# DeltaNet phase: products kept for the other direction, decays and triangles of two steps made in the tail of the step before

## The reference

```
S_t = exp(g_t)(I - beta_t k_t k_t^T) S_{t-1} + beta_t k_t v_t^T ;  o_t = S_t^T q_t
o_f, s_f = gated_delta_scan(dq, dk, dv, beta[:, :, 0], g[:, :, 0], dn_s0[:, 0])
o_b, s_b = gated_delta_scan(flip(dq), flip(dk), flip(dv), flip(beta[:, :, 1]), flip(g[:, :, 1]), dn_s0[:, 1])
o_dn = o_f + flip(o_b)
```

## Time and profile before

| | |
|---|---|
| median of 3 runs | 3465.98 us (3464.9 to 3468.81) |
| the profiled execution | 3469.74 us |
| its span in the trace | 3468.0 us |
| TensorE, VectorE, ScalarE, GpSimd busy | 3281.3, 2291.9, 1768.7, 298.5 us |
| step 1 of the DeltaNet phase, first turn to first turn | 1447.26 to 1511.61 |
| first turn of step 0; the next phase's start | 1388.43; 1699.95 |

### The profile page before, as it was taken

The page is one execution under the profiler, slowest core; times in us unless marked ns, Lnnn a source line. Parts: engine busy times, 40 slices in busy tenths (PEclk is TensorE's granted clock), DMA queues, the critical chain, the costliest instruction groups (busy, mean ns, idle before and its releaser), DMA issues. The chain is left out here.

```text
span 3468.0 us, 48349 instructions
## 1 busy us (share of the span) xinstructions
PE 3281.3 (95%) x19680; PEld 2709.8 (78%) x19680; DVE 2291.9 (66%) x2436; ACT 1768.7 (51%) x2260; POOL 298.5 (9%) x302
## 2 busy tenths in 40 slices
PE   5899998999999999999979999959999999999995
PEld 0799998989999998999869998846666666666663
DVE  1587547656665666445574352678888888888886
ACT  2455323323433233666573233537777777777774
POOL 0000000001100001311212000010000100100000
PEclk8999999999999999999989999979999999999997
DMA  9422323545455553312436333869999999999998
GB/s 414 164 91 84 148 111 123 178 165 187 169 185 185 177 184 107 77 38 74 122 86 211 121 132 134 308 228 349 390 399 396 376 395 398 386 384 395 396 372 324
DMA packets 176358, 794.42 MB, mean 229 GB/s; under 512 B 17460, under 2 KB 70068, under 8 KB 96948
## 3 DMA queue, kind: packets, MB, share of 16 engines
q1 hardware_dynamic: 158180, 699.81, 54.0%
q0 software_dynamic: 17136, 86.91, 7.6%
q10 hardware_dynamic: 864, 5.27, 0.4%
HBM read 729.48 MB, written 62.46 MB: 228 GB/s over the span
## 5 line engine op out<-in xcount | busy, mean ns | idle before, releaser
L2557 DVE TENSOR_TENSOR expert_lo<-expert_ring,first_expert_hi 128x2048 fp32r<-128x2048 f32 x288 | 660.0, 2292 | 111.7 <-ACT first_expert_hi L2494 108.0
L2494 ACT ACTIVATE first_expert_hi<-expert_ring 128x2048 fp32r<-128x2048 f32 x285 | 546.9, 1919 | 175.0 <-PE bank L2441 175.0
L2440 PE MATMUL bank<-expert_lo,xeT_hi 128*80 128x512 f32 x1024 | 402.1, 393 | 0.0
L472 PE MATMUL bank<-h_hi,part_hi 128*128 128x320 f32 x960 | 301.6, 314 | 8.2 <-DVE part_lo_x L860 4.5
L2439 PE MATMUL bank<-first_expert_hi,xeT_hi 128*80 128x512 f32 x768 | 303.2, 395 | 1.2 <-DVE xeT_lo L2562 1.2
L2441 PE MATMUL bank<-first_expert_hi,xeT_lo 128*80 128x512 f32 x768 | 299.2, 390 | 0.0
L472 PE MATMUL bank<-h_lo,part_hi 128*128 128x320 f32 x960 | 298.2, 311 | 0.0
L860 DVE TENSOR_TENSOR part_lo_x<-part_x,part_hi 128x1024 fp32r<-128x1024 f32 x120 | 149.3, 1245 | 152.7 <-ACT part_hi L684 145.5
L2557 DVE TENSOR_TENSOR expert_lo<-expert_ring,expert_hi 128x2048 fp32r<-128x2048 f32 x96 | 219.6, 2287 | 43.5 <-ACT expert_hi L2494 43.5
L684 ACT ACTIVATE part_hi<-part_x 128x1024 fp32r<-128x1024 f32 x120 | 127.3, 1061 | 217.3 <-PE bank L472 197.6
L472 PE MATMUL bank<-s_hi,part_hi 128*128 128x320 f32 x720 | 226.7, 315 | 4.0 <-DVE part_lo_x L860 4.0
(11 more groups left out here) (406 smaller groups left out, 7630.5 us busy)
## 6 DMA issues: line engine op xcount, KB each, us to landing
expert_ring<-d_wgate SPq DMA_DIRECT2D x128, 1024.0 KB, 7.3
expert_ring<-d_wup_e SPq DMA_DIRECT2D x128, 1024.0 KB, 7.8
expert_ring<-d_wdown SPq DMA_DIRECT2D x128, 1024.0 KB, 10.3
mod_slot<-d_wmod SPq DMA_DIRECT2D x56, 1024.0 KB, 6.7
part_b<-d_win SPq DMA_DIRECT2D x90, 512.0 KB, 3.2
front_ring<-d_wmod SPq DMA_DIRECT2D x40, 1024.0 KB, 8.3
front_ring<-d_win SPq DMA_DIRECT2D x29, 1024.0 KB, 4.8
d_proj<-out_rows POOLq DMA_DIRECT2D x86, 320.0 KB, 2.4
```

The costliest lines, as they stand in the source:

```text
L472: mm = pe.matmul(part_bank[j][:, 0:HALF_T], w, a[:, kk, :], start=(kk == 0 and x == 0), stop=(kk == HALF_K - 1 and x == 2))
L2440: pe.matmul(out[0:CAP, :], a_hi, lo, start=False, stop=False)
L2494: act.activation(w_hi[n % NSPLIT][:], w[:, n % NSLOT].rearrange("p (k n) -> p k n", n=HALF), ACT.Copy).then_inc(s["we_high"], 1)
L2557: dve.tensor_tensor(w_lo[n % NSPLIT][:], w[:, n % NSLOT].rearrange("p (k n) -> p k n", n=HALF), w_hi[n % NSPLIT][:].bitcast(F32), ALU.subt ...
```

## The change

- Step 0 makes kT, vT, KK and QK once for both directions (quads 0 and 2). VectorE does the halves of level 0 of a pair straight behind its triangles.
- Steps 1 and 2 make them for all four quads. ScalarE then copies KK out of PSUM into `keys_keys` (which takes R's place) and QK into `vnew`, eight copies of 128x512. The triangles read `keys_keys`, and scoresT reads `vnew` and is made behind the halves of level n = 2. R is written over `vtok`.
- SP stores V, KK and QK of step 1 and V and QK of step 2 in HBM (`d_keep`, 20 DMAs of 256 KB), and brings them back for the other direction: V and QK of step 2 in step 3, the three of step 1 in step 4 (20 DMAs). KK of step 2 stays in SBUF. Values are fetched no more for steps 3 and 4.
- Steps 3 and 4 leave out kT, vT, KK and QK. Their decay rows, decays, triangles and first strips are made in the tail of the step before (EARLY_HEADS): the decay rows behind XTend on TensorE, the decays behind the XT copies on ScalarE, the triangles between R and the O/S updates on VectorE. QS of quads 1 and 3 is done ahead of the levels.

The diff, cut to its core:

```diff
+def dn_left_out(q):
+
+    return {FIRST_STEP: ("QS", "KS", *(FRESH if q % 2 else ())), 3: FRESH, LAST_STEP: (*FRESH, "S")}
+EARLY_HEADS = (3, 4)
...
+                for q in range(4):
+                    B[q].wait_emptied(sp, 1, "vT")
+                    keep(KEEP_V1, q, vtok)
+                for q in range(4):
+                    A[q].wait_emptied(sp, 1, "KK")
+                    keep(KEEP_KK1, q, KK)
+                for q in range(4):
+                    B[q].wait_emptied(sp, 1, "QK")
+                    keep(KEEP_QK1, q, vn)
+                next_keys(2)
...
+                next_keys(3)
+                sp.wait_ge(spilled, SPILLED[2])
+                for q in range(4):
+                    A[q].wait_filled(sp, 2, "P")
+                    bring(KEEP_V2, q, vtok, v_back)
+                for q in range(4):
+                    A[q].wait_filled(sp, 2, "O")
+                    bring(KEEP_QK2, q, vn, qk_back)
+                for p in range(2):
+                    sp.wait_ge(LT_made[p], 4)
+                for q in range(4):
+                    bring(KEEP_KK1, q, KK, kk_back)
+                next_keys(4)
...
                             if n == 1:
-                                A[2 * p].wait_emptied(pool, step, "KK")
-                                A[2 * p + 1].wait_emptied(pool, step, "KK")
+                                pool.wait_ge(LT_made[p], step + 1)
...
+                    fresh = {0: QUADS[0::2], 1: QUADS, 2: QUADS}.get(step, ())
...
+                    if step not in EARLY_HEADS:
+                        decay_rows(step)
...
+                    if not fresh:
+                        for q, d, h0 in QUADS[1::2]:
+                            wait_rows(step, d, landed)
+                            queries_state(step, q, d, h0, x)
...
                         turn(A[q], step, "XTend", lambda h: (E, O)[d][p][0][:, h, :])
+                    if step + 1 in EARLY_HEADS:
+                        decay_rows(step + 1)
...
+                    for q in range(4 if step in (1, 2) else 0):
+                        A[q].wait_filled(act, step, "KK")
+                        act.activation(KK[q][:], h4(A[q].t[:]), ACT.Copy).then_inc(A[q].emptied, 1)
+                    for q in range(4 if step in (1, 2) else 0):
+                        B[q].wait_filled(act, step, "QK")
+                        act.activation(vn[q][:], h4(B[q].t[:]), ACT.Copy).then_inc(B[q].emptied, 1)
...
+                    if step + 1 in EARLY_HEADS:
+                        decays(step + 1)
+                    if step in SPILLED:
+                        act.wait_ge(spilled, SPILLED[step])
...
+                def triangles(step, p):
+                    for q, d, h0 in QUADS[2 * p:2 * p + 2]:
+                        if step == FIRST_STEP:
+                            A[q - d].wait_filled(dve, step, "KK")
+                            keys = h4(A[q - d].t[:])
+                        else:
+                            if step < 3:
+                                A[q].wait_emptied(dve, step, "KK")
+                            elif step == 4:
+                                dve.wait_ge(kk_back, 64)
+                            keys = KK[keys_of(step, q)][:]
+                        A[q].wait_emptied(dve, step, "G")
+                        for h in range(4):
+                            c = d * 8 + h0 + h
+                            op = dve.scalar_tensor_tensor(
+                                out=NT[p][:, 1 - d, h, :], in0=keys[:, h, :],
+                                scalar=col(k.beta[:], tile_at(step, d), c, c + 1), in1=DT[q][:, h, :],
+                                op0=ALU.mult, op1=ALU.mult)
+                    if step == FIRST_STEP:
+                        op.then_inc(A[2 * p].emptied, 1)
+                    dve.drain().then_inc(LT_made[p], 1)
+                    cut(dve, p, 0).then_inc(first_strip[p], 1)
...
+                        if step > FIRST_STEP and n == 2:
+                            for q, d, h0 in QUADS:
+                                if step < 3:
+                                    B[q].wait_emptied(dve, step, "QK")
+                                else:
+                                    dve.wait_ge(qk_back, 64 * (step - 2))
+                                dve.tensor_tensor(sc[q][:], vn[q][:], DT[q][:], ALU.mult)
...
+                            if step < 3:
+                                dve.wait_ge(spilled, SPILLED[step])
+                            else:
+                                dve.wait_ge(v_back, 64 * (step - 2))
...
                     dve.drain()
+                    if step + 1 in EARLY_HEADS:
+                        for p in range(2):
+                            triangles(step + 1, p)
```

More of the change, by code:

```diff
@@ L85, with __init__ @@
 class Bank:
-    def __init__(self, tensor, filled, emptied, fills, left_out):
+    def __init__(self, tensor, filled, emptied, names):
         self.t, self.filled, self.emptied = tensor, filled, emptied
-        names = [(step, f) for step in range(TT) for f in fills if f not in left_out.get(step, ())]
         self.before = {name: n for n, name in enumerate(names)}
@@ L103, in wait_emptied, with in_steps @@
         wait(eng, self.emptied, self.before[step, fill] + 1)
+def in_steps(fills, left_out):
+    return [(step, f) for step in range(TT) for f in fills if f not in left_out.get(step, ())]
 class Chip:
@@ L985, with a_names @@
 FIRST_STEP, LAST_STEP = 0, TT - 1
[L986 removed]
+FRESH = ("kT", "vT", "KK", "QK")
+KEEP_V1, KEEP_KK1, KEEP_QK1, KEEP_V2, KEEP_QK2 = range(5)
+def dn_left_out(q):
+    return {FIRST_STEP: ("QS", "KS", *(FRESH if q % 2 else ())), 3: FRESH, LAST_STEP: (*FRESH, "S")}
 B_FILLS = [["vT", "QK"] + [f"XY{s}" for s in LEVELS[1:]] + ["QS", "S"], ["vT", "QK", "QS", "S"]]
+EARLY_HEADS = (3, 4)
+def a_names(q):
+    names = in_steps(A_FILLS[q % 2], dn_left_out(q))
+    for step in EARLY_HEADS:
+        names.remove((step, "G"))
+        names.insert(names.index((step - 1, "XTend")) + 1, (step, "G"))
+    return names
 def columns(ap, s, other, heads=P):
@@ L1015, in phase_deltanet @@
         ktok, vtok, DT, sc = (quads(n) for n in ("ktok", "vtok", "decayT", "scoresT"))
-        XT, R, vn, vs = (quads(n) for n in ("XT", "R", "vnew", "vweighted"))
+        XT, KK, vn, vs = (quads(n) for n in ("XT", "keys_keys", "vnew", "vweighted"))
         NT = [sb(f"LT{p}", [P, 2, 4, P]) for p in range(2)]
@@ L1075, in _, with keep @@
                              ).then_inc(k.ml_first_in, 16)
[L1076 to L1083, removed]
+                def keep(slot, q, src):
+                    sp.dma_start(k.d_keep[slot, q], src[q][:].rearrange("p h n -> p (h n)")).then_inc(spilled, 16)
@@ new lines, in bring, with next_keys @@
+                def bring(slot, q, dst, back):
+                    sp.dma_start(dst[q][:].rearrange("p h n -> p (h n)"), k.d_keep[slot, q ^ 1]).then_inc(back, 16)
+                def next_keys(step):
+                    for d in range(2):
+                        sp.wait_ge(used[d], step * 2)
+                        fetch(step, (step, TT - step), d, 0, 16, landed)
+                for d in range(2):
+                    B[2 + d].wait_filled(sp, 1, "vT")
+                    fetch(2, (2, TT - 2), d, 16, 24, v_landed)
@@ L1124, in turn, with wait_rows, queries_state, decay_rows @@
                     mm.then_inc(bank.filled, 1)
[L1126 to L1137, removed]
+                def wait_rows(step, d, arrived):
+                    pe.wait_ge(arrived[0 if step == FIRST_STEP else d], 16 if step == FIRST_STEP else 16 * (step + 1 - d))
+                def queries_state(step, q, d, h0, x):
+                    fill(B[q], step, "QS", lambda h: [(staged[d][:, h0 + h, :], S[x][q][:, h, :])])
+                def decay_rows(step):
                     for q, d, h0 in QUADS:
@@ new lines, in body @@
+                    for p in range(2):
+                        if step not in EARLY_HEADS:
+                            triangles(step, p)
+                        if step == FIRST_STEP:
+                            halves(step, 0, p)
+                    for n in range(len(LEVELS)):
+                        for p in range(2):
+                            if step > FIRST_STEP or n > 0:
+                                halves(step, n, p)
+                        if step == FIRST_STEP and n == 0:
+                            for q, d, h0 in QUADS:
+                                B[q - d].wait_filled(dve, step, "QK")
+                                op = dve.tensor_tensor(sc[q][:], h4(B[q - d].t[:]), DT[q][:], ALU.mult)
+                                if d == 1:
+                                    op.then_inc(B[q - 1].emptied, 1)
+                        if step > FIRST_STEP and n == 2:
[5 more added lines that the diff above has]
+                                dve.tensor_tensor(sc[q][:], vn[q][:], DT[q][:], ALU.mult)
```

137 lines of the change are left out of this document (77 added, 60 removed).

## The result

The changed kernel takes 3483.42 us (median of 5, 3483.01 to 3485.3), the kernel before, beside it, 3466.59: ratio 1.0049, interval 1.0037 to 1.0062. It is slower by 17 us; forecast were 3466.6 and a range up to 3475. The profiled execution has a span of 3481.2, of before 3468.0.

What follows compares the result with a forecast made beforehand. TensorE was taken to set the pace, with VectorE the bound in the changed tails of steps 3 and 4. Gains of 11.0 us less 9.8 for VectorE-GpSimd meetings and 1.8 for clock gave -0.6: median 3466.6, range 3455 to 3475.

Steps and rivals of the forecast that it cites:

- The triangles of the second pair wait for one strip at most: VectorE's second-pair triangles, steps 1 to 4, wait for one GpSimd strip over SBUF: 1.2 us each, 4.8 together.
- The carry copies: Steps 3 and 4: four VectorE copies meet GpSimd's back-to-back strips, two passing per gap: 1.7 us a step, 3.4 together.
- second rival: GpSimd retakes the port after every VectorE instruction; copies and scores wait a strip each: 9.2 us slower, 3475; chance 0.17.
- The clock: TensorE's gaps in the heads of steps 3 and 4 lower its clock: 1.8 us for one head, bounds 0 and 3.6.
- a sign that all of it is wrong: The whole forecast is wrong if the six levels no longer take 30.85 us.
- Step 0: Sixteen turns and 16 products go, ScalarE has four copies fewer: gain 1.5 us, bounds 0 and 2.7.
- the interleaving: Step 0: second pair's triangles stand some 1.4 us behind the first pair's turn and halves; some 1.0 less after the last strip.
- Steps 1 and 2: First level begins later because ScalarE copies KK behind the decays: a loss of 1.1 us each, 2.2 together.
- the 2.0 us of KK behind the decays: Steps 1 and 2: triangles start 2.0 us later, as ScalarE's first KK copy comes after the decays.
- The scores: Steps 1 and 2: free in second-level gaps at 2.48 us; meeting GpSimd's strips costs 0.8 each, 1.6 together, bounds 0 to 2.0 each.
- Steps 3 and 4 without contention: XTend's end to first level takes 26.95 us, from 33.5 into step 3: gains 6.55 and 4.8, together 11.4.
- Transfers: Added 256 KB DMAs and dropped v fetches cost nothing, each issued at least 20 us ahead of use.

Runs made afterwards that it cites:

- second run: Changed kernel with GpSimd's strips started only behind VectorE's first strip of the second pair: 3476.65 us, ratio 1.0030 to the kernel before.
- first experiment: Changed kernel with GpSimd's first strip of a pair waiting for VectorE's strip of that same pair: 3476.34 us, ratio 1.0029 to the kernel before.
- third run: Changed kernel with the four carry copies of steps 3 and 4 moved to the begin of the tail before: 3473.36 us, ratio 1.0022.
- fifth: Changed kernel with GpSimd behind both VectorE strips and the carry copies at the begin of the tail before: 3462.15 us, ratio 0.9989.
- sixth: The fifth run's kernel; in steps 1 and 2 triangles read KK from PSUM and scores come behind level 3: 3453.99 us, ratio 0.9966.
- ninth run: The eighth run's kernel plus two fills of unread products on TensorE between step 0's two XY1 turns: 3448.91 us, ratio 0.9948.
- seventh run: The sixth run's kernel with step 0's halves of level 0 behind both pairs' triangles again: 3454.02 us, ratio 0.9966.
- eighth run: The seventh run's kernel; VectorE adds the state's part of quads 1 and 3 to o_dn during levels 1 and 2, steps 3 and 4: 3450.79 us.
- repetition: The eighth run's kernel measured once more, unchanged: 3450.92 us.

## Why the prediction was wrong

**The step that failed** is "The triangles of the second pair wait for one strip at most ... 1.2 in each of four steps, 4.8". I had the resource right and the meeting wrong. GpSimd is released by the triangles, ahead of VectorE's own strip, and got the port first; so both of VectorE's strips wait, in every step, step 0 too, 1.15 each (to the next start: 1460.45 to 1462.33 is 1.88, 1456.71 to 1457.44 was 0.73): 11.5 us, not 4.8. The triangles waited for nothing (2.17). Without these waits the heads were 9.1 us shorter (second run, the cast left aside). I read in the earlier trace rows that GpSimd's strip waited for VectorE's and did not ask what the 0.05 us that set this order would be after the edit. The first experiment puts the wait where I had forecast it, at about 1.1 in each of four steps. The Trainium skill's rule (SBUF — State Buffer, "Who interferes with whom") has it that whoever issues first keeps the port for a whole instruction; GpSimd's strip of 1.31 and VectorE's of 1.95, with starts 0.01 apart, agree.

**The carry copies** were the right place at half the price: 4.45 us for 0.85, so 3.6 a head, where I took 1.7. Moving them away shortened the two heads by 8.0 us in all, their own time included (third run). GpSimd let one copy by at a time; that was the second rival's mechanism, and its 3.9 was near. Its 3475 still was 8 too low, for want of the strips.

**The clock** was charged once, 1.8 us. The first level became longer in all five steps, together 6.7; the prediction had named levels that are no longer 30.85 as a sign that all of it is wrong. I had looked for gaps in the heads of steps 3 and 4 alone. They came in steps 0 to 2 as well, and the late strips widened them: TensorE waited 4.97, 3.48 and 3.48 us there for the second pair's first strip, and 3.80, 1.41 and 1.41 in the second run. Each gap closed by an edit gave its levels 30.8 again (third, fifth, sixth and ninth run).

**Step 0**: forecast 1.5 faster; the head is 1.7 slower, 1.25 from the first turn on. Two strips wait (2.3), and the interleaving costs 1.5 in the head (seventh run), where I had counted 1.4 less 1.0. Without both, the head is 1.7 faster than before the change (21.86 for 23.58), near the forecast. Behind it come 1.0 more in the levels at the lower clock.

**Steps 1 and 2**: the 2.0 us of KK behind the decays was right (triangles 9.28 behind the first turn, 7.20 before) and came back in the sixth run. The first level, for which I counted 1.1 a step, came 1.9 later in the second run, where TensorE also waited 0.78 for GpSimd's first strip. The scores cost nothing in the change, in step 1 by 0.16 us; where they meet the strips they take 2.75 and 2.43 longer, above the 2.0 of my bound, and TensorE waits 1.50 and 1.18 of it.

**Steps 3 and 4 without contention**: forecast 26.95 for the stretch, 26.1 without the copies' 0.85; 25.86 in the fifth run, where the copies are out of it. The early heads and the missing products are worth what was counted, and the collisions ate it.

**Transfers**: nothing, as forecast. No wait of the phase in the trace ends with one of them, and of the edits that gave the time back none touched them, but for KK's return, which is released one strip later.

## What to carry to other kernels

When a change moves an instruction of VectorE that reads two tiles of SBUF, or a copy, into a stretch in which GpSimd works, price it at a whole GpSimd instruction for each one that is met, and look which of the two is released first, down to hundredths of a microsecond. A release that stands one instruction too early can cost about what the change saves: here 9 us in the heads, where the early heads, freed of the meetings, are worth 10. Releasing GpSimd only when VectorE's last such instruction is done cost 0.9 us in step 0, and in the last versions nothing in the others; look what else it then meets, as the scores did in the second run. Then look for the gaps that such waits open on TensorE, in every step, since what follows can be paid at a lower clock.

## What was not expected of the hardware

- The start of VectorE's and GpSimd's strips lay 0.05 us apart before and 0.01 the other way after, and the later one paid: 0.6 us (GpSimd) or 1.1 (VectorE).
- Behind a train of strips VectorE's copies of 0.3 us advance by one per strip, 1.27 apart, while VectorE's O/S updates in the same train, with one input in PSUM, keep their 0.67 and 1.11 us.
- A gap of about 2 us on TensorE did not always cost: the same program's levels of step 0 took 30.82 us in one execution, behind a gap of 1.97 us, and 31.80 in another, behind 2.12 (eighth run and its repetition).
- The same cast of VectorE beside the same memsets of GpSimd was held for 3.76 us in some executions and for 4.22 in others, one further memset of 0.5 us, and the start of the phase moves with it.
